# Nine query weight tiles loaded ahead of the first gather, and ScalarE's opening order

## What is computed

```python
merged = g_a * (o_a @ w_br_a[l]) + g_b * (o_b @ w_br_b[l]) + g_c * (o_c @ w_br_c[l])
x = x + merged @ w_out[l]
x = x + peer_ffn(rmsnorm(x, ln2_w[l]), peer_wq[l], peer_subkeys[l], peer_u[l], peer_v[l])

def peer_ffn(...):                      # per token, 8 heads
    q = zb @ wq                         # 1024 -> 8 heads x 2 halves x 128
    s = einsum('thpd,hpnd->thpn', q, subkeys)      # 128 scores per half
    # top 16 of each half, top 16 of the 256 sums: 16 experts of 16384 per head
    h = einsum('thkd,td->thk', u_tab[expert], zb)
    act = gate * gelu(h)
    return einsum('thk,thkd->td', act, v_tab[expert])
```

## Time and profile before

| what | us |
|---|---|
| median of three runs | 3999.93 |
| profiled execution, its own time | 4001.03 |
| span of that execution | 3999.2 |
| PE busy | 3676.3 |
| DVE busy | 2564.7 |
| ACT busy | 1599.3 |
| POOL busy | 684.0 |
| first layer: first gather issued | 2250.12 |
| first layer: last dot product begins | 2909.98 |
| second layer: first gather issued | 3321.96 |
| second layer: last dot product begins | 3981.72 |

### The profile page before, as it was taken

One profiled execution on the slowest core, in us unless ns is written; L12 is line 12 of the kernel. 1 busy time (PEld: TensorE's weight loads), 2 busy tenths in 40 slices (PEclk: granted clock), 3 DMA queues, 4 the chain that ended last, 5 costly groups with the idle time before them and its releaser, 6 DMA issues. The chain is left out here.

```text
span 3999.2 us, 66179 instructions
## 1 busy us (share of the span) xinstructions
PE 3676.3 (92%) x25476; PEld 3168.1 (79%) x25476; DVE 2564.7 (64%) x5169; ACT 1599.3 (40%) x3560; POOL 684.0 (17%) x698
## 2 busy tenths in 40 slices
PE   8999989999999998999899999888889999988887
PEld 6888766788788876898778898777777798987776
DVE  4878547677755566655456767776563567677774
ACT  4222537323332344443235444444332454444443
POOL 0110002000000002000000244444300003444442
PEclk9999999999999999999999999999999999999999
DMA  6555211355433420454135699999942257999998
GB/s 243 199 188 189 78 53 53 106 186 184 146 116 139 146 85 22 174 185 169 65 107 189 257 420 420 420 420 420 421 157 87 104 212 322 420 420 421 420 420 333
DMA packets 135482, 911.58 MB, mean 228 GB/s; under 512 B 14839, under 2 KB 16119, under 8 KB 34048
## 3 DMA queue, kind: packets, MB, share of 16 engines
q0 software_dynamic: 93952, 615.72, 38.0%
q1 hardware_dynamic: 41216, 291.63, 20.0%
HBM read 906.21 MB, written 5.28 MB: 228 GB/s over the span
## 5 line engine op out<-in xcount | busy, mean ns | idle before, releaser
L2793 PE MATMUL ps<-arena 128*128 128x128 f32 x6560 | 837.1, 283 | 150.6 <-ACT arena L2856 150.3
L2793 PEld LDWEIGHTS ps<-arena 128*128 128x128 f32 x6560 | 789.8, 196 | 205.6 <-ACT arena L2856 199.3
L2981 DVE CUSTOM_DVE_ANT_0 arena<-arena 128x1024 f32<-128x1024 f32 x410 | 502.4, 1226 | 306.0 <-DMA arena<-peer_uv,arena 304.5
L698 DVE TENSOR_TENSOR w_lo<-wt,w_hi 128x1024 fp32r<-128x1024 f32 x389 | 476.6, 1225 | 313.1 <-ACT w_hi L680 286.3
L2953 POOL DMA_INDIRECT arena<-peer_uv,arena x410 | 438.1, 1068 | 1393.9 <-DVEq L2921 803.5
L733 PE MATMUL ps<-h_hi,w_hi 128*128 128x512 f32 (+1 forms) x1744 | 643.6, 371 | 14.0 <-ACT h_hi L904 9.3
L680 ACT ACTIVATE w_hi<-wt 128x1024 fp32r<-128x1024 f32 x389 | 408.8, 1061 | 581.6 <-PE ps L733 547.2
L733 PE MATMUL ps<-h_hi,w_lo 128*128 128x512 f32 (+1 forms) x1744 | 633.8, 365 | 0.0
L733 PE MATMUL ps<-h_lo,w_hi 128*128 128x512 f32 (+1 forms) x1744 | 593.0, 365 | 0.3 <-DVE h_lo L940 0.3
L733 PEld LDWEIGHTS ps<-h_hi,w_hi 128*128 128x128 f32 x1744 | 330.7, 190 | 72.7 <-issue 9.7
L733 PEld LDWEIGHTS ps<-h_hi,w_lo 128*128 128x128 f32 x1744 | 330.6, 190 | 54.6 <-issue 1.9
(11 more groups left out here) (351 smaller groups left out, 5290.8 us busy)
## 6 DMA issues: line engine op xcount, KB each, us to landing
wt<-wstream SPq DMA_DIRECT2D x253, 1024.0 KB, 4.9
ada_t<-adastream POOLq DMA_DIRECT2D x128, 512.0 KB, 3.6
arena<-wstream SPq DMA_DIRECT2D x12, 1024.0 KB, 7.0
arena<-adafirst SPq DMA_DIRECT2D x8, 1024.0 KB, 15.4
arena<-peer_uv,arena POOLq DMA_INDIRECT x410, 19.9
arena<-bias_by_query POOLq DMA_DIRECT2D x2, 3072.0 KB, 15.0
bias_by_query<-bias_by_distance POOLq DMA_DIRECT2D x1, 4096.0 KB, 16.9
xT<-tokens SPq DMA_DIRECT2D x2, 1024.0 KB, 6.4
```

The costliest lines, as they stand in the source:

```text
L698: self.step(self.dve.tensor_tensor(lo, raw_group(g), hi.bitcast(F32), ALU.subtract))
L2793: ins = pe.matmul(y_banks(t)[m // 4][:, (m % 4) * P:(m % 4 + 1) * P], row[:, D + m * P:D + (m + 1) * P], diag[n % DIAGS], start=s == 0 and ...
L2981: dve.tensor_tensor_reduce(u, u, ztok[:, t], 1.0, 0.0, ALU.mult, ALU.add, hbuf[:, t, s:s + 1]).then_inc(dot_ready.sem, 1)
```

## The change

Five things:

1. **Plan.** All eight columns of `w_out` stand together (four ring tiles), and the queries begin on a new tile. A layer's expert weights are now nine tiles instead of the end of the old order.
2. **Six of the nine stand aside.** The first three go to arena places of the last three row buffers (`IN_ROWS`), the next three to the bias place. SP issues the first three between the loads of `w_out`, after a wait on `gated`, which DVE raises at the last gated product of the merge. The last three of the nine go through the ring.
3. **Row buffers** are reordered, so that the three that hold weights come last in each layer; gathers 7, 8 and 9 of a layer wait for `aside_used`, which PE raises as it is done with each of the three tiles. The number of buffers stays ten.
4. **`pe_merge`** no longer jumps, and owes nothing at its end.
5. **Opening.** ACT writes chunk k + 1 (`tokens`) before it copies strip k + 2 and splits the next weights.

Cut to its core:

```diff
@@ weight_plan
-        square("w_out", l, range(0, D - 2 * P, P))
+        square("w_out", l, range(0, D, P))
+        align()
         square("peer_wq", l, [0, P])
-        square("w_out", l, range(D - 2 * P, D, P))
         for i in range(2):
             add("peer_subkeys", l, 0, i * P)
-        align()
...
-ASIDE = {PLAN.index((*first, width)) // W_TILE + i: 3 * n + i
-         for l in range(2) for n, (first, width) in enumerate(((("nsa_ck_w1", l, 0, 0), 2), (("peer_wq", l, 0, 2 * P), 1)))
-         for i in range(3)}
+ASIDE = {PLAN.index((*first, width)) // W_TILE + i: at + i
+         for l in range(2) for first, width, at, n in ((("nsa_ck_w1", l, 0, 0), 2, 0, 3), (("peer_wq", l, 0, 0), 1, 3, 6))
+         for i in range(n)}
...
+        aside += [arena[:, (10 + i) * W_TILE * P:(11 + i) * W_TILE * P] for i in range(3)]
         aside += [arena[:, i * W_TILE * P:(i + 1) * W_TILE * P] for i in range(3)]
...
+                    if ASIDE.get(self.tile) in IN_ROWS:
+                        self.used += 1
...
+                elif W.used and not start:
+                    ins.then_inc(aside_used, 1)
+                    W.used -= 1
@@ act_first_norm
-            for k in range(DC):
+
+            def tokens(k):
                 act.wait_ge(xn_ready.sem, xn_ready.due(act))
                 act.wait_ge(mod_set, k + 1)
                 step(modulate(act, 0, 0, T, k))
                 act.activation(h_hi[:, k, 0:T], hT[:, k, 0:T], ACT.Copy).then_inc(h_hi_ready.sem, 1)
+
+            tokens(0)
+            for k in range(DC):
+                if k + 1 < DC:
+                    tokens(k + 1)
                 if k + 2 < DC:
                     act_strip(act, step)
                 if k < DC - BEGUN:
@@ pe_merge
-                if m == DC - 2:
-                    W.go_to("w_out", l, 0, m * P)
...
-            W.go_on_behind("peer_subkeys", l, 0, P, owed=2)
+            W.go_on_behind("peer_subkeys", l, 0, P, owed=0)
+            W.used = 1
@@ dve_merge
+                    if n == N_MERGE - 1:
+                        dve.sem_inc(gated, 1)
@@ row buffers
+        E_.at = 12 * P * DC
         rows = [E_(2 * D) for _ in range((ARENA - E_.at) // (2 * D))]
-        rows += [a[:, :, :].rearrange("p a b -> p (a b)") for a in (ada_t, silu_cc)]
+        rows = [*rows[:4], rows[7], *(a[:, :, :].rearrange("p a b -> p (a b)") for a in (ada_t, silu_cc)), *rows[4:7]]
@@ pool_peer
+                if GB - len(IN_ROWS) <= at < GB:
+                    pool.wait_ge(aside_used, base // N_SLOTS * len(IN_ROWS) + at - GB + len(IN_ROWS) + 1)
@@ sync
+                        m = PLAN.index(("peer_wq", l, 0, 0, 1)) // W_TILE + i
                         if NTH[n] == merge_at[l] + W_SLOTS + 2 * (i + 1):
-                            m = PLAN.index(("peer_wq", l, 0, 2 * P, 1)) // W_TILE + i
+                            sp.dma_start(aside[6 + i], wstream[m + 3]).then_inc(aside_full[6 + i], 16)
+                        if NTH[n] == out_at[l] + 2 + i:
+                            sp.wait_ge(gated, l + 1)
                             sp.dma_start(aside[3 + i], wstream[m]).then_inc(aside_full[3 + i], 16)
```

More of the change, by code:

```diff
@@ L414, in model_kernel @@
         w_full = [sem(f"w_full{i}") for i in range(W_SLOTS)]
-        aside_full = [sem(f"aside_full{i}") for i in range(6)]
+        aside_full = [sem(f"aside_full{i}") for i in range(9)]
         aside = [arena[:, ARENA - (i + 1) * W_TILE * P:ARENA - i * W_TILE * P] for i in range(3)]
+        aside += [arena[:, (10 + i) * W_TILE * P:(11 + i) * W_TILE * P] for i in range(3)]
         aside += [arena[:, i * W_TILE * P:(i + 1) * W_TILE * P] for i in range(3)]
+        aside_used = sem("aside_used")
         w_free = sem("w_free")
@@ L461, in reached @@
                 self.eng.wait_ge(self.chain, n)
+        IN_ROWS = (3, 4, 5)
         class Weights:
             def __init__(self, pe):
-                self.pe, self.at, self.owed, self.tile = pe, 0, 0, None
+                self.pe, self.at, self.owed, self.tile, self.used = pe, 0, 0, None, 0
             def next(self, *key, width=1):
@@ L684, in model_kernel, with __init__ @@
         class SplitLo:
-            def __init__(self, dve, step, groups, begun=0, ahead=SPLITS, kept=None):
-                self.dve, self.step, self.left, self.kept = dve, step, list(groups)[begun:], kept
+            def __init__(self, dve, step, groups, begun=0, ahead=SPLITS):
+                self.dve, self.step, self.left = dve, step, list(groups)[begun:]
                 for _ in range(ahead - begun):
@@ L699, in ahead @@
                     self.dve.sem_inc(split_ring.full, 1)
-                    if (g % 2 or self.left and self.left[0] > g + 1) and g != self.kept:
+                    if g % 2 or self.left and self.left[0] > g + 1:
                         self.dve.sem_inc(w_free, 1)
@@ L2470, in merge_groups @@
         def merge_groups(l):
-            g = groups_of("w_br_a", l, (M_STEPS + DC + 2) * P)
-            return [*g[:-4], *g[-2:]]
+            return groups_of("w_br_a", l, (M_STEPS + DC) * P)
         def gated_by(n):
@@ L2630, in dve_merge @@
         def dve_merge(dve, step, l):
-            weights = SplitLo(dve, step, merge_groups(l), ahead=1, kept=merge_groups(l)[-1])
+            weights = SplitLo(dve, step, merge_groups(l), ahead=1)
             for n, (whole, hi, lo) in enumerate(TO_SPLIT):
@@ L2685, in model_kernel @@
         E_ = Carve(B0)
+        gated = sem("gated")
         token_ready = signal("token_ready")
@@ L2785, in pe_peer @@
                 for s in range(h * PEER_K, (h + 1) * PEER_K):
-                    row = rows[n % GB]
+                    row = rows[(n - l * N_SLOTS) % GB]
                     if scoring:
@@ L2946, in pool_peer @@
         def pool_peer(pool, base):
-            for n, (t, s) in enumerate((t, s) for t in range(QT) for s in range(SLOTS)):
-                n += base
+            for at, (t, s) in enumerate((t, s) for t in range(QT) for s in range(SLOTS)):
+                n = base + at
                 if s % PEER_K == 0 or (t, s) == (0, PEER_K // 2):
                     pool.wait_ge(experts_ready.sem, experts_ready.due(pool))
+                if GB - len(IN_ROWS) <= at < GB:
+                    pool.wait_ge(aside_used, base // N_SLOTS * len(IN_ROWS) + at - GB + len(IN_ROWS) + 1)
                 if n >= GB:
                     pool.wait_ge(row_free, n - GB + 1)
-                pool.indirect_dma_start(out=rows[n % GB], out_offset=None, in_=peer_uv,
+                pool.indirect_dma_start(out=rows[at % GB], out_offset=None, in_=peer_uv,
                                         in_offset=bass.IndirectOffsetOnAxis(ap=experts[:, t, s:s + 1], axis=0)
@@ L2978, in dve_peer @@
                 for s in range(h * PEER_K, (h + 1) * PEER_K):
-                    u = rows[n % GB][:, 0:D]
+                    u = rows[(n - base) % GB][:, 0:D]
                     dve.wait_ge(row_full[n % GB], 16 * (n // GB + 1))
@@ L3178, in _ @@
             merge_at = [NTH[PLAN.index(("w_br_a", l, 0, 0, 1)) // W_TILE] for l in range(2)]
+            out_at = [NTH[PLAN.index(("w_out", l, 0, 0, 1)) // W_TILE] for l in range(2)]
             layer_at = PLAN.index(("peer_subkeys", 0, 0, (2 * PEER_H - 1) * P, 1)) // W_TILE + 1
```

## The result

| | before | after |
|---|---|---|
| median, us (5 runs each) | 4002.32 | 3980.66 |
| range of the runs | 3998.0 to 4004.12 | 3978.45 to 3983.36 |
| span of the profiled execution | 3999.2 | 3979.0 |
| first layer: first gather issued | 2250.12 | 2243.76 |
| first layer: from there to the last dot product | 659.86 | 651.31 |

The ratio is 0.9946, 95% interval 0.9935 to 0.9957. The spans differ by 20.2 us, the medians by 21.7; 22.5 had been predicted. Span and distances split the 20.2 into 6.36 before the first gather, 8.55 and 6.94 in the two gather stretches, and a loss of 1.6 between the layers.

The account below looks back on a forecast made before the run. PE was taken to bound most of the kernel, full DMA the last third of each layer. Opening 7.3 plus gathers 15.2 over two layers, other terms 0, made 22.5 off 3999.93: 3977.4 us, range 3970 to 3987.

Parts of the forecast that it names:

- The opening: First chunks: modulating chunk k + 1 earlier removes six PE waits for ACT's `h_hi`, gaining 7.3 us.
- The w_out stretch: Output product `w_out`: added weight loads hide under PE and the wait on `gated` costs 0, with 9 us margin.
- The new waits of POOL: Gather 9 waits for PE to leave the third tile, issued 3.3 us later; cost 0, margin 8 us.
- theory A: One-tile run: the DMA hole behind gather 9 is idle time from late gathers 9 and 10; distance stays 651 to 653.
- The gathers: Expert rows: five tiles moved out relieve DMA by 8.9 us, limited by 9.2 us landing to 7.6 per layer.
- The sum: Whole kernel: 7.3 + 15.2 = 22.5 us gained, median 3977.4; chance 0.52.
- the opening is given back: Rival: the opening's gain is lost in the feed-forward part behind it; 15.2 remain, 3984.7 us; chance 0.13.
- the heads set the pace: Rival: landings can't get shorter than gather 90's 16.8, so layers gain nothing; 7.3 remain, 3992.6 us; chance 0.08.
- whole transfers: Rival: in the gathers every moved tile is worth its full 2.5 us; 32.3 gained, 3967.6 us; chance 0.05.
- slower: Rival: SP stands on `gated`, the last `w_out` tile lands late; 17 us lost per layer, 4011; chance 0.04.
- The latency of an empty queue doesn't bind: Rival: in the gathers the relief is the full 8.9 per layer; 25.1 gained, 3974.8 us; chance 0.18.

Follow-up runs that it names:

- the run with one tile: Changed kernel with only the ninth expert-weight tile held until PE has left the third tile aside, when gather 9 is issued: 3983.27 us, 0.9951 of the kernel before.
- the second execution: The changed kernel itself, unaltered, run and profiled again: 3983.86 us, 0.9948 of the kernel before.
- the buffer experiments: Nine row buffers instead of ten, in the changed kernel (3985.07 us, 0.9960 of before) and in the kernel before (4003.16 us, 1.0006).
- the opening alone: The kernel before with only ACT's new opening order: 3995.21 us, 0.9982 of the kernel before.
- the weights alone: The changed kernel with ACT's old opening order: 3990.94 us, 0.9969 of the kernel before.
- the two kernels with tiles held to gather 9: Changed kernel with all three ring tiles (3986.04 us, 0.9957 of before) or only the ninth tile (3983.27 us, 0.9951) held to gather 9.

## Why the prediction was right, and where its terms were off

**The opening, 7.3.** All six waits went. The chunk's period fell to 6.51, not to the 6.64 that was read as its work: (7.85 - 6.51) x 6 = 8.0 us. At the first gather 6.36 were left in the first execution. That loss is not one of the mechanism: first gathers stand at 2241.8 to 2244.2 in the seven executions with the new opening (mean 2243.0) and at 2250.1 to 2252.8 in the three without (mean 2251.6), 8.6 apart, with a spread of some 2.5 us in each group. The term was about 1 us too small, which is less than that spread.

**The w_out stretch, 0.** Held. PE is busy for 25.94 of 26 us, and the last of the seven loads is out at 2222.7.

**The new waits of POOL, 0.** Held. The wait came, and later than forecast: gather 9 is 4.8 us behind its turn at 16.2 - 11.4, not 3.3. Of the other 1.5 us, 1.35 are idle time ahead of PE's fourth half (1.94 in place of 0.59). It stands at 2259.97 in a layer whose gathers begin 6.36 earlier than before, so against the margin of 2272.5 - 6.4 = 2266 it was in time. The step let DMA come to gather 9 some 27 us behind the first gather, which counts 5 us to the first packet; with the weight tiles gone the packets are there sooner, and nine gathers' bytes had moved at 25.2 us. Even so gather 9, issued at 16.2, held nothing up. The stretches of the changed kernel show DMA full until 2270, 26.2 us behind the first gather; it falls as the packets of gather 9 run out and gather 10, issued at 2270.65, has none yet.

```profile
2268.00:2270.00 2.00, 2.00 (x12) 2.00 (x11) 1.90 (x8) 0.75 (x3) 0.00 (x0) 0.50 1.03 430
2270.00:2272.00 2.00, 2.00 (x9) 1.82 (x9) 1.93 (x6) 0.90 (x3) 1.09 (x1) 0.50 0.52 217
2272.00:2274.00 2.00, 2.00 (x16) 1.95 (x16) 1.97 (x5) 0.18 (x1) 0.01 (x1) 0.85 0.74 193
```

So the hole belongs to gather 10, which waits for PE's first row, and not to gather 9, which theory A of the run with one tile names beside it. It makes 362 GB/s in the first 46 us against 410 before, and its cost is in the next step.

Whole first 46 us and the rest of the gathers, of the kernel before and of the changed one, in the columns of the earlier trace rows:

```profile
2250.00:2296.00 46.00, 39.30 (x257) 35.54 (x256) 37.39 (x114) 18.04 (x59) 19.53 (x19) 0.96 0.99 410
2296.00:2909.00 613.00, 524.66 (x4099) 491.13 (x4099) 416.47 (x1000) 265.95 (x810) 255.57 (x237) 0.98 1.01 417
```

```profile
2244.00:2290.00 46.00, 38.85 (x242) 35.02 (x241) 39.02 (x117) 16.18 (x54) 18.66 (x19) 0.93 0.93 362
2290.00:2895.00 605.00, 521.85 (x4114) 490.76 (x4112) 414.27 (x995) 264.07 (x818) 263.34 (x238) 0.98 1.01 417
```

**The gathers, 7.6 per layer.** Measured 8.55 and 6.94, then 6.4 and 5.5 in the second execution, where row 0 was later. The size was right, the reason was not, and that the two came out near each other is in part luck. The forecast let the relief end where issue to landing can't get shorter, at 9.2. Gather 90 did land about there: the last increment of its semaphore stands 9.8 and 9.0 us behind its issue in the two layers, in the second execution 9.7 and 9.6. But its dot product in the first layer begins 0.9 us later than that, behind DVE's own work, so the landing is no longer what it needs. And 9.2 is not what an empty queue takes: gather 10, issued as DMA ran dry, landed 5.9 and 6.1 us behind its issue, where 8 to 9 had been forecast.

What sets the relief is bytes less idle time. Five tiles freed are 12.5 us, and DMA idles for (410 - 362) x 46 / 420 = 5.3 us more than before; the difference is 7.2, against 8.55 measured, and rates given to whole GB/s, over stretches cut to whole us, leave the rest open. So it is the issue of gather 10 and of those behind it, each waiting for a row of PE's, that holds the relief below 12.5, and the buffer experiments show that issue now binds.

In the first us the gather queue was faster than forecast, too: it had moved 1.59 MB by 6.2 us behind the first issue, more than the bytes of one gather.

```profile
q0 software_dynamic: 210, 1.59, 64.1%
```

This row is 2243 to 2250 us. The 5 us to the first packet that the earlier trace rows seemed to show were for the most part the weight tiles ahead: in the changed kernel the gather queue moved 0.77 MB within 4.2 us of its first issue.

```profile
q0 software_dynamic: 94, 0.77, 49.5%
```

This row is 2243 to 2248 us. The Trainium skill, DMA: Bandwidth & Descriptors, section "Anatomy of one DMA", with its 2.0 us plus bytes, gives 4.4 us for one gather. The trace has 0.77 MB after 4.2 us, less than one gather, and gather 10 landed at 5.9: above the page's figure, and well below the 9.2 that the forecast preferred to it.

**The sum.** 22.5 forecast; 20.2 between the profiled spans, 21.7 and 20.2 between medians in the two comparisons. By the mean first gathers the opening brought about 1 more than forecast (in the first execution, at 6.36, about 1 less), and the first layer about 1 more. The second layer brought 0.7 less in the first execution, and 1.6 were lost between the layers, of which no part of the change is shown to be the cause; the same stretch, 412.0 us before, was 411.8 with the opening alone, 412.4 with the weights alone, and 413.6 and 415.9 in the two executions of the changed kernel. Of the rivals "the opening is given back", "the heads set the pace", "whole transfers" and "slower" are excluded by the runs. "The latency of an empty queue doesn't bind" was right in what it says of the latency and wrong in its time, since the late issue of gather 10 took the place of latency.

## What to carry to other kernels

A transfer moved out of a stretch in which DMA is full is worth its bytes less the idle time that the emptied queue then shows, so ask which issue comes late once the queue is short; here gather 10's wait for PE's first row was hidden before and is paid for after. Idle DMA time behind such a point is free room: one load of 2.5 us put there cost nothing, three cost 2.3 to 3.8 us (both read against the line of row 0). Where two profiled executions of one kernel differ by 2 us, compare stretches only against the quantity that moves them, here the start of the first row.

## What was not expected of the hardware

- The granted clock fell from 2.4 to 1.2 GHz around PE's wait for the first row, in both kernels, and stayed down longer after the change. Before, PE was idle for 4.34 us and the clock stood at 1.2 GHz from 2272.2 to 2275.6; after, PE was idle for 3.43 us and it stood there from 2265.8 to 2272.6. So rows 0 and 1 took 3.78 and 2.70 us on PE instead of 3.51 and 1.95. Row 2 begins 30.2 us behind the first gather, before 28.4: that is the 1.8 by which the heads start later, 0.4 of it already there at row 0. The same drop of 0.74 in 2262 to 2275 us stands in the two kernels with tiles held to gather 9, so in the first layer it makes no difference among them. No run shows why it lasts longer.

```profile
2272.53 3.51 PE L2793 MATMUL ps<-arena 128*128 128x128 f32 x16 [4.34 <-ACT arena L2856]
...
2276.31 1.95 PE L2793 MATMUL ps<-arena 128*128 128x128 f32 x16
```

```profile
2266.60 3.78 PE L2809 MATMUL ps<-arena 128*128 128x128 f32 x16 [3.43 <-ACT arena L2872]
...
2271.02 2.70 PE L2809 MATMUL ps<-arena 128*128 128x128 f32 x16
...
2273.99 1.95 PE L2809 MATMUL ps<-arena 128*128 128x128 f32 x16
```

- A gather of 1 MB issued as DMA runs dry landed in 5.9 us (gather 10 after the change), a third of the 16.8 that gather 90 took amid full DMA before it.
- The same program, executed twice, gave distances 2.1 and 1.4 us apart, and PE's semaphore for a query half came up to 1.7 us later than usual.
